# A hybrid decoder step on one core: residual rows turned by VectorE with short store runs, scores and splits in another order

## What is computed

```
h = rmsnorm(x); proj = h @ w_in                 # q,k,v,z_A,alpha,beta,u,z_B
o_a = gated delta rule (8 heads of 128)         # half of the mixing width
o_b = causal pooling over 2/4/8/16 positions    # the other half
x  = x + concat(o_a, o_b) @ w_out               # x2, the residual rows
h2 = rmsnorm(x); qx = h2 @ w_cq                 # 4 heads of 512
scores = qx @ mem_k; probs = softmax(scores)    # 256 memory tokens
x  = x + (probs @ mem_v) @ w_co
y  = rmsnorm(x)
```

## Time and profile before

| | |
|---|---|
| three runs, us | 1635.26, 1636.34, 1639.36 (median 1636.34) |
| profiled execution, us | 1636.29 |
| its span, first to last instruction, us | 1634.5 |
| busy in the span | PE 98%, PEld 88%, DVE 60%, ACT 40%, POOL 10% |
| granted TensorE clock, mean | 0.995 |
| DMA | 274.65 MB, mean 168 GB/s |

### The profile page before, as it was taken

One profiled execution on the slowest core, in us unless ns is written; L12 is line 12 of the kernel. 1 busy time (PEld: TensorE's weight loads), 2 busy tenths in 40 slices (PEclk: granted clock), 3 DMA queues, 4 the chain that ended last, 5 costly groups with the idle time before them and its releaser, 6 DMA issues.

```text
span 1634.5 us, 29970 instructions
## 1 busy us (share of the span) xinstructions
PE 1597.5 (98%) x12034; PEld 1441.9 (88%) x12034; DVE 978.8 (60%) x1669; ACT 647.0 (40%) x1110; POOL 155.7 (10%) x170
## 2 busy tenths in 40 slices
PE   7999999999999999999999999999999999999997
PEld 5887899999999999999999999999999996667655
DVE  5676447776857767667344563434688765532445
ACT  5666444343543434425322233323434325332422
POOL 0121000211121121211100011111000000000000
PEclk9999999999999999999999999999999999999999
DMA  7798744332342332424289946777613359977664
GB/s 270 247 293 260 238 132 119 79 94 75 97 111 60 99 98 70 115 52 131 77 194 232 248 134 169 221 217 217 166 57 99 104 175 335 333 246 250 222 222 161
DMA packets 318832, 274.65 MB, mean 168 GB/s; under 512 B 17402, under 2 KB 266115, under 8 KB 317715
## 3 DMA queue, kind: packets, MB, share of 16 engines
q1 hardware_dynamic: 296304, 256.48, 52.8%
q10 hardware_dynamic: 22434, 16.87, 3.8%
HBM read 229.49 MB, written 44.17 MB: 167 GB/s over the span
## 4 chain that ended last, share of the span: by engine, by line
PE 96%; DVE 2%; ACT 1%; DMA 0%; issue 0%; SPq 0%; ACTq 0%; DVEq 0%
PE pj L283 51%; PE pj L504 11%; PE dk L2998 6%; PE pj L2338 4%; PE dk L2338 3%; PE pj L2957 3%; PE pj L2965 2%; PE dk L2623 1%; DVE w_low_co L2557 1%; PE pj L2645 1%; PE pj L2662 1%; PE dk L1926 1%; PE dk L1303 1%; PE dk L366 1%; PE dk L1319 1%; PE dk L1419 1%
## 5 line engine op out<-in xcount | busy, mean ns | idle before, releaser
L283 PE MATMUL pj<-a_hi,w_high 128*128 128x272 f32 x1664 | 364.7, 300 | 0.0
L283 PE MATMUL pj<-a_hi,w_low 128*128 128x272 f32 x1664 | 343.6, 288 | 0.0
L283 PE MATMUL pj<-a_lo,w_high 128*128 128x272 f32 x1664 | 343.1, 288 | 0.0
L283 PEld LDWEIGHTS pj<-a_hi,w_high 128*128 128x128 f32 x1664 | 259.4, 189 | 12.3 <-issue 7.8
L283 PEld LDWEIGHTS pj<-a_lo,w_high 128*128 128x128 f32 x1664 | 261.5, 188 | 0.0
L283 PEld LDWEIGHTS pj<-a_hi,w_low 128*128 128x128 f32 x1664 | 260.0, 189 | 0.0
L267 DVE TENSOR_TENSOR w_low<-w_raw,w_high 128x2048 fp32r<-128x2048 f32 x68 | 155.3, 2284 | 85.4 <-ACT w_high L257 85.4
L257 ACT ACTIVATE w_high<-w_raw 128x2048 fp32r<-128x2048 f32 x68 | 130.4, 1917 | 75.1 <-PE pj L283 42.4
L283 PE MATMUL pj<-mix_hi,w_high 128*128 128x272 f32 x512 | 107.1, 290 | 0.0
L283 PE MATMUL pj<-mix_lo,w_high 128*128 128x272 f32 x512 | 105.7, 288 | 0.0
L283 PE MATMUL pj<-mix_hi,w_low 128*128 128x272 f32 x512 | 105.3, 287 | 0.0
(11 more groups left out here) (464 smaller groups left out, 2913.8 us busy)
## 6 DMA issues: line engine op xcount, KB each, us to landing
w_raw<-in_w_in_dram SPq DMA_DIRECT2D x48, 1024.0 KB, 6.0
w_raw_co<-in_w_co_dram SPq DMA_DIRECT2D x28, 1024.0 KB, 6.9
w_raw_wide<-in_w_ck_dram SPq DMA_DIRECT2D x16, 1024.0 KB, 9.6
w_raw_wide<-in_w_cv_dram SPq DMA_DIRECT2D x16, 1024.0 KB, 7.8
w_raw<-in_w_out_dram SPq DMA_DIRECT2D x16, 1024.0 KB, 7.9
keys_s<-keysT_scratch SPq DMA_DIRECT2D x7, 2048.0 KB, 10.7
values_s<-in_cache_mem_v_dram SPq DMA_DIRECT2D x28, 512.0 KB, 7.0
q_part<-in_w_cq_dram SPq DMA_DIRECT2D x48, 256.0 KB, 3.6
```

The costliest lines, as they stand in the source:

```text
L283: mm = pe.matmul(pj[:, 2 * (q % 2) + b, 0:n], wt[:, k, :], x(k, o, n), start=(k == 0 and m == 0), stop=(k == KT - 1 and m == 2))
```

## The change

1. *Residual rows.* PE's transposes (turn_x2), ACT's copies (act_x2) and the semaphore x2_taken are gone. DVE turns x2's 512 prompt columns in 32x32 blocks into xr, behind the requests' transpose. sp_x2 stores xr with four DMAs a tile, one for each 32 partitions, in runs of 32 floats. The residual load of tile i + 2 waits until tile i's store from the same buffer has landed (64 a tile on x2_stored), not for the sum's read. All later waits on x2_stored go from 128 to 512.
2. *Banks.* The scores of head 3 lie in dk banks 0 and 1, and wait for pt_low of head 0 only.
3. *Order of attention.* PE: scores 3 and the turn of head 2 go ahead of the requests' values of head 0, and the turn of these goes into unit 0. ACT and DVE: turned values of head 0 and 1 and weight tiles 0 and 1 are prepared earlier.
4. *Order of the products.* DVE splits tile w + 1 ahead of both products of w, and makes a request head's sums and the next head's queries ahead of products or rows. ACT takes the requests' context of head 0 between the products of tile 0.

```diff
@@ -1995,7 +1995,7 @@
             if 4 * j + q >= 2:
-                sp.wait_ge(pj_read, 80 + 4 * j + q - 1)
+                sp.wait_ge(x2_stored[q % 2], 64 * (2 * j + q // 2))
             sp.dma_start(xr[q % 2][:], xT_d[bass.ds(4 * j + q, 1), :, :].rearrange("k p n -> p (k n)")).then_inc(xr_loaded[q % 2], 16)
@@ -2017,30 +2017,15 @@
-            sp.wait_ge(x2_taken, i + 1)
-            sp.dma_start(x2_d[:, :, i * P:(i + 1) * P].rearrange("b p c -> p b c"),
-                         x2[i % 2][:, 0:SEQ].rearrange("p (b c) -> p b c", b=CH)).then_inc(x2_stored[i % 2], 16)
+            sp.wait_ge(x2_turned, i + 1)
+            rows = x2_d[:, :, i * P:(i + 1) * P].rearrange("n (q t) (a f) -> a t (n q) f", t=T32, f=T32)
+            for a in range(4):
+                sp.dma_start(rows[a], xr[i % 2][a * T32:(a + 1) * T32, 0:SEQ].rearrange("t (b f) -> t b f", f=T32)).then_inc(
+                    x2_stored[i % 2], 16)
             if i % 4 == 3:
...
                     sp.dma_start(x2s_d[:, i - 3:i + 1, a, :], xs_t[i // 4 % 2][a * NS:(a + 1) * NS]).then_inc(x2s_stored, 16)
-
-        def turn_x2(i, bank):
-
-            def step(pe):
-                pe.wait_ge(pj_read, 80 + i + 1)
-                at_least(pe, x2_taken, i - 3)
-                for b in range(CH):
-                    mm = pe.transpose(dk[:, bank, b * P:(b + 1) * P], x2[bank % 2][:, b * P:(b + 1) * P], ident)
-                mm.then_inc(x2_turned, 1)
-            return step
-
-        def act_x2(act, i):
-
-            act.wait_ge(x2_turned, i + 1)
-            act.wait_ge(h_low, i + 1)
-            act.wait_ge(sqx_ready, i + 1)
-            act.activation(x2[i % 2][:, 0:SEQ], dk[:, i % 4, :], ACT.Copy).then_inc(x2_taken, 1)
@@ -2050,8 +2035,6 @@
                     i = 4 * j + q
-                    if i > 0:
-                        act_x2(act, i - 1)
                     act.wait_ge(pj_read, 80 + i + 1)
@@ -2074,7 +2057,7 @@
                     dve.wait_ge(xr_loaded[q % 2], 32 * j + 16 * (q // 2) + 16)
-                    at_least(dve, x2_stored[q % 2], 32 * j + 16 * (q // 2))
+                    at_least(dve, x2_turned, i - 1)
                     at_least(dve, sqx_ready, i - 1)
@@ -2086,6 +2069,8 @@
                     dve.transpose(xs_t[j % 2][:, q, :], x2[q % 2][:, SEQ:TOK]).then_inc(xs_turned, 1)
+                    dve.wait_ge(pj_read, 80 + i + 1)
+                    dve.transpose(xr[q % 2][:, 0:SEQ], x2[q % 2][:, 0:SEQ]).then_inc(x2_turned, 1)
             for j in range(4):
@@ -2114,12 +2099,10 @@
                     pe.wait_ge(ust_ready, 8)
-                if q > 0:
-                    steps = {7: [turn_x2(q - 1, q - 1)]}
                 multiply(pe, "out", 0, q, tokens(mix_hi), tokens(mix_lo), TOK, steps)
...
                 for q in range(4):
-                    multiply(pe, "out", j, q, tokens(mix_hi), tokens(mix_lo), TOK, {7: [turn_x2(4 * j + q - 1, (q - 1) % 4)]})
+                    multiply(pe, "out", j, q, tokens(mix_hi), tokens(mix_lo))
@@ -2233,7 +2216,7 @@
                 for k in range(2):
-                    dve.wait_ge(x2_stored[k], 128)
+                    dve.wait_ge(x2_stored[k], 512)
                 dve.wait_ge(x2s_stored, 256)
@@ -2317,7 +2300,6 @@
                     pe.wait_ge(col2_root, 1)
-                    pe.wait_ge(x2_taken, 16)
             elif kh == 0 and o == 0:
@@ -2364,8 +2346,6 @@
                     cast_high(act, "cq", 0, q + 1)
-                if q == 0:
-                    act_x2(act, 15)
                 if q == 1:
@@ -2427,7 +2407,6 @@
             pe.wait_ge(acc_done, 16)
-            pe.wait_ge(x2_taken, 14)
             for i in range(4):
@@ -2435,7 +2414,7 @@
             multiply(pe, "cq", 0, 0, tokens(a_hi), tokens(a_lo), TOK,
-                     {7: [turn_x2(15, 3)], 14: [lambda pe: pe.wait_ge(h_low, 16)], 15: [lambda pe: token_sums(pe)]})
+                     {14: [lambda pe: pe.wait_ge(h_low, 16)], 15: [lambda pe: token_sums(pe)]})
             for q in range(1, 4):
@@ -2609,15 +2588,15 @@
-            return (dk[:, 0:2, :], dk[:, 2:4, :], pj[:, 0:2, :], dk[:, 2:4, :])[h]
+            return (dk[:, 0:2, :], dk[:, 2:4, :], pj[:, 0:2, :], dk[:, 0:2, :])[h]
...
             if h == 3:
-                pe.wait_ge(pt_high.sem, pt_high.at(2))
-                pe.wait_ge(pt_low.sem, pt_low.at(2))
+                pe.wait_ge(pt_high.sem, pt_high.at(1))
+                pe.wait_ge(pt_low.sem, pt_low.at(1))
             for i in range(4):
@@ -2680,11 +2659,10 @@
             pe_turn(pe, 1)
+            pe_prompt_scores(pe, 3)
+            pe_turn(pe, 2)
             pe_values(pe, 0, 0)
             pe_values(pe, 0, 1)
-            pe_prompt_scores(pe, 3)
-            pe_turn_values(pe, 0)
-            pe_turn(pe, 2)
@@ -2748,12 +2726,13 @@
             act_exps(act, 2)
-            act_values(act, 0)
             act_turned_values(act, 0)
             cast_product(act, 0)
-            act_context(act, 0)
             act_turned(act, 2)
             act_exps(act, 3)
+            act_values(act, 0)
+            act_turned_values(act, 1)
+            cast_product(act, 1)
@@ -2803,9 +2782,10 @@
             maxima(3)
+            split_product(dve, 0)
             dve_turned(dve, 2)
             over_sums(3)
-            split_product(dve, 0)
+            dve_turned_values(dve, 1)
@@ -2874,9 +2854,9 @@
                 w = TILE_UNITS.get(u)
-                if w is not None and w + 1 < TILES:
+                if w is not None and 1 < w + 1 < TILES:
                     cast_product(act, w + 1)
-                if u < XH - 1:
+                if 0 < u < XH - 1:
                     act_turned_values(act, u + 1)
@@ -2887,9 +2867,11 @@
                 if w is not None:
+                    if w == 0:
+                        act_turned(act, 3)
                     act_product(act, w, 0)
                     if w == 0:
-                        act_turned(act, 3)
+                        act_context(act, 0)
                     act_product(act, w, 1)
@@ -2920,21 +2902,21 @@
                 if step == 2:
                     probabilities(dve, h)
-                if u < XH - 1:
+                if 0 < u < XH - 1:
                     dve_turned_values(dve, u + 1)
-                if w is not None:
-                    dve_product(dve, w, 0)
-                    if w == 0:
-                        dve_turned(dve, 3)
-                    if w + 1 < TILES:
-                        split_product(dve, w + 1)
-                    dve_product(dve, w, 1)
-                else:
-                    dve_rows_unit(dve, u)
+                if w is not None and w + 1 < TILES:
+                    split_product(dve, w + 1)
                 if step == 1:
                     request_sums(dve, h)
                     if h + 1 < XH:
                         queries(dve, h + 1)
+                if w is not None:
+                    if w == 0:
+                        dve_turned(dve, 3)
+                    dve_product(dve, w, 0)
+                    dve_product(dve, w, 1)
+                else:
+                    dve_rows_unit(dve, u)
         def pe_products(pe):
@@ -3005,10 +2987,10 @@
                     if w == 0:
+                        pe_turn_values(pe, 0)
                         high_half(w, 1)
+                        pe_turn(pe, 3)
                     low_half(w, 0)
-                    if w == 0:
-                        pe_turn(pe, 3)
                     if AGAIN <= w + 1 < TILES:
```

More of the change, by code:

```diff
@@ L1964, in build @@
             "h_high", "h_low", "sqx_ready", "acc_zero", "acc_done"))
-        x2_turned, x2_taken, xs_turned, x2s_stored = (sem(n) for n in ("x2_turned", "x2_taken", "xs_turned", "x2s_stored"))
+        x2_turned, xs_turned, x2s_stored = (sem(n) for n in ("x2_turned", "xs_turned", "x2s_stored"))
         xs_t = [put(f"xs_t{i}", [4, NS], F32, M_W - 272 + i * 4 * NS) for i in range(2)]
@@ L2350, in sp_cq @@
             for i in range(2):
-                sp.wait_ge(x2_stored[i], 128)
+                sp.wait_ge(x2_stored[i], 512)
             sp.wait_ge(sums_done, 1)
@@ L2815, in build @@
         gain_loaded, xs_loaded = Reused(old_rows, 16), Reused(mst_stored, 128)
-        x_half_loaded = [Reused(x2_stored[i], 128) for i in range(2)]
+        x_half_loaded = [Reused(x2_stored[i], 512) for i in range(2)]
         (out_done, row_added, row_squared, row_summed, row_root, row_over, row_gained, row_scaled_a, row_scaled_v, s_added) = (
@@ L3161, in sp_rows_out @@
             for s, v in ((mst_stored, 128), (kts_stored, 128), (xts_stored, 80), (st_stored, 768), (s_stored, 128),
-                         (s0_stored, 128), (ust_stored, 16 * 72), (old_rows, 16), (x2_stored[0], 128), (x2_stored[1], 128),
+                         (s0_stored, 128), (ust_stored, 16 * 72), (old_rows, 16), (x2_stored[0], 512), (x2_stored[1], 512),
                          (x2s_stored, 256)):
```

## The result

The changed kernel takes **1621.73 us** (median of 4 runs, 1620.14 to 1623.8), the kernel before beside it 1635.8 (4 runs, 1635.1 to 1639.36): a ratio of 0.9911, interval 0.9899 to 0.9923. The forecast was 1618 in a range of 1608 to 1630. The profiled execution took 1621.54 us, 1.7 more than its span.

The account below looks back on a forecast made before the run. PE was taken to bound the kernel, busy 1597.5 of 1634.5 us. Terms -7.0 - 5.4 - 3.4 - 3.2 + 0.6 = -18.4 took 1636.3 to 1618 us, range 1608 to 1630.

Parts of the forecast that it names:

- Part 1, PE's work: Output and query stages: PE loses 64 transposes, sixteen groups of 0.44 us, for -7.0 us.
- Part 1, the added wait: Output stage: residual load waits for the store's landing, about one us late, unseen by PE; price 0, bounds 0 and +15.
- the slack of 3.7 us: Output stage: time free between the end of DVE's low-part split and PE's need for it, 3.7 us.
- second rival: Output stage: loads landing 26.5 us behind the add delay each tile pair 2.5 us; 15 us, 1633 us; chance 0.22.
- Its milder reckoning: Output stage, second rival: one us lost per pair of tiles instead of 2.5, for 1622 us.
- Part 2: Output tiles 12 to 15: split first closes three 1.80 us waits, -5.4 us; half-clock stretches disappear, -3.4 us.
- Part 3: Later attention units: requests' sums first closes two of three waits for probabilities, -3.2 us.
- Part 4: Turn from attention to products: waits close, but late weights 3 cost PE 5 to 7 us; +0.6 instead of -9.1.
- first rival: Turn to products: the queue makes up its delay, loads aren't late, part 4 brings -9.1; 1608 us; chance 0.18.
- third rival: Output stage: 128-byte writes cost 54 ns beside weight loads, DMA sets the stage, +43 us; 1668 us; chance 0.06.
- the turning point: Output stage, third rival: the change turns slower at 39 ns a packet, where a tile needs over 13.15 us.
- fourth rival: DVE's new order exposes another equal wait and the clock falls; only part 1 left, 1629 to 1634; chance 0.06.

Follow-up runs that it names:

- Split first alone: Kernel before with only DVE's split of tile w + 1 ahead of both products of w, for w from 1 on: 1628.1 us, ratio 0.9943.
- the sums alone: Kernel before with only DVE's requests' sums and next head's queries ahead of products or rows: 1630.96 us, ratio 0.9956.
- (store): Changed kernel with SP storing a tile's turned residual rows before it waits for the turned keys: 1619.32 us, ratio 0.9899.
- (residual load): Changed kernel with the residual load issued ahead of the weight load, from the second tile on: 1618.59 us, ratio 0.9883.
- (weights 2): Changed kernel with weights 2 and turned values 3 loaded ahead of head 1's first keys: 1619.75 us, ratio 0.9905.
- (rows): Changed kernel with the 2 MB load of residual rows behind weights 3 instead of ahead: 1616.58 us, ratio 0.9878.
- all together: Changed kernel with residual load before weights, store before keys, weights 2 and values 3 before head 1's keys, 2 MB rows behind weights 4: 1608.07 us, ratio 0.982.
- part 1 alone: Kernel before with only the block transposes in the out stage, old attention order: 1632.1 us, ratio 0.997.

## Why the prediction was right, and where it was off

**The sum.** -3.3 + 1.7 - 3.6 - 9.6 = -14.8 against -18.4: right in sign and in the range, 3.7 us too good. One term of part 1 has all of it. The other misses, +1.1 in part 4, -0.4 in part 3 and -0.8 in part 2, cancel each other, and that is luck.

**Part 1, PE's work: right.** Sixteen groups at 0.44 us were to bring 7.0; with the loads in time the run gave 7.1.

**Part 1, the added wait: the step that failed** is "one us late. PE doesn't see it ... Price 0". It measured 3.85 us. In the round shown the way to the load was right within 0.2 us (store 14.5 us behind the sum for 14.65, load at 20.1 for 20.1). Two things were not. The load took 6.1 us beside the weights, so it landed at 26.2 and not at 25. And the slack of 3.7 us was charged once, though the lateness of one round is handed to the next: against a grid of 12.0 us from the first sum (979.90), the sums of tiles 5, 7 and 9 came 1.3, 2.3 and 4.6 us late (1041.20, 1066.18, 1092.47), and with the third the slack was used up. A loop whose rounds are longer than their period on average has no slack; it only takes a number of turns to show.

That is the second rival's mechanism, with 3.85 us in place of its 15. Its round of 26.5 us was nearly right for a long round (26.3 and 26.8), but it took every round to be one, and the others took 23.8 to 25.0: over the five rounds from tile 5 on the mean is 25.2. Only two tiles made PE stand. Its milder reckoning, one us a pair, gave 7.5 - 3.7 = 3.8 us and 1622, and 3.85 and 1621.7 came, closer than the 2 us to which this term is known, so in part luck. So the outcome is the forecast's for parts 2 to 4 and for PE's work in part 1, and the second rival's for the added wait.

**Part 2: right, by both of its terms.** Split first alone gave 9.4 us from tile 12 on, waits and clock together; forecast 5.4 + 3.4.

**Part 3: right.** Forecast 3.2, measured 3.6; the sums alone remove the three waits.

**Part 4: the mechanism right, one size off.** The keys load left 3.3 us later than before, at 1377.64; in the time of the kernel before (3.3 us are part 1's) that is 1380.9, forecast 1381.1. Weights 3 landed at 1405.2 + 3.3 = 1408.5, forecast 1407.5, and PE started tile 3 at 1412.8, forecast 1411.6. The mis-sized term is the share of the delay that the queue would make up: 1.3 of 6.8 us were allowed for, 0.3 came. From the issue of the keys load to the landing of weights 3 it was 27.5 us, as before (27.7: 1374.32 to 1402.0), with the same 7.5 MB of loads between them; with the 2 MB of rows moved behind weights 3 it was 22.4.

The clock fell twice, where one stretch was forecast, but the first (from 1396.1) lay ahead of the long wait and only made that wait shorter: it cost nothing. The second, from 1406.3 to 1413.2, overlapped 3.7 us of work behind the wait and cost half of it, 1.8 us, for 1.7. The first rival (loads not late) fell with the 5.56 us wait; orders that land weights 3 earlier against the first scores, after 65.6, 62.9, 60.4 and 56.5 us, bring the request turn after 77.1, 74.3, 73.0 and 67.3 us, so the landing sets it, except that at 60.4 another wait had taken over. By that row most of that rival's -9.1 was there to be had: 67.3 is 8.1 less than the 75.4 of before.

**The third rival fell.** DMA queues from 1000 to 1100 us, to be read against the earlier trace rows:

```profile
q1 hardware_dynamic: 42528, 16.87, 68.0%
q10 hardware_dynamic: 6730, 4.11, 15.0%
```

The share grew by 7.3 and 0.7 points, not to near 1. The first queue's 7.3 points are 7.3% x 16 x 100 / 8.33 = 14.0 us of engine time a tile; with the removed 512 packets at the mix's 33 ns (an estimate) the 2048 new ones took (14.0 + 16.9) / 2048 = 15 ns each beside weight loads, where 39 (38 by its own terms) would have been the turning point. The rule that was weighed there, from the Trainium skill, "DMA: Bandwidth & Descriptors", Specifications (under 512 bytes not at line rate), gives no size; here the rows show such packets at 13 ns almost alone and, by that estimate, 15 beside weight loads. The mix before moved 16.71 MB in 29689 packets, 563 bytes each, in 33 ns, so a byte in a 128-byte packet took 1.7 to 2 times as long (an estimate): the direction of the rule is borne out, and the output stage didn't feel it: with the residual load ahead of the weights its tiles last 12.00 us.

**The fourth rival fell** with the last window of the result: no PE wait and the full clock from 1413.2 to 1614.

## What to carry to other kernels

When a change makes a buffer serve twice (load, store, load again), write down the whole round, from use to use, and compare it with the period; if it is longer by one microsecond on average, slack of four is spent in four rounds, so never charge it once. Count what comes only every few turns too. Of loads on one queue, put those that are wanted soonest and are smallest first: 272 KB behind 1 MB took twice as long to land, and 2 MB that nobody needed yet held up 1 MB that PE was waiting for. And before an instruction is moved on a compute engine, look which load waits for it and how full the queue is behind that load.

## What the runs showed beyond what was expected

- **The order of issues was worth as much as the change.** The same work with the DMA issues in another order went from 1621.7 to 1608.1 us. By the ratios to the kernel before, the single edits gave 2.0 (store), 4.6 (residual load), 1.0 (weights 2) and 5.4 us (rows) over the changed kernel; each ratio is known to some 2 us, so the first and the third are not clear of noise as times. The sum of the two of the attention stage and the larger of the other two is 11.0, less than the 14.9 of all together (where the rows go one load further back, and no stretch at 1.2 GHz is left).
- **A full queue.** Weights 3, 1 MB, landed 18.0 us after their issue in the changed kernel and 9.1 in the kernel before, though the DMA share was 1.04 between issue and landing in both; they were issued 2.4 us earlier than there (1387.17 + 3.3 against 1392.8) and landed 6.5 us later. The other orders gave 19.7, 16.7 and 13.3 us at shares of 1.02 to 1.04. So the share doesn't tell when a load lands; what is still ahead of it does. The same 7.5 MB stood ahead of weights 3 in both kernels, from the keys load on, issued within 9.5 us in the changed one and 18.5 before.
- **The same wait, another clock.** A wait of 2.4 us in tile 0 was followed by a stretch at 1.2 GHz in the kernel before and by none with part 1 alone, and the three waits of 1.80 us by two such stretches in the kernel before, with the sums first and with part 1 alone. The wait of 1.83 us in tile 1, with the splits first, and those of 1.96 us for the probabilities were followed by none. So the clock's share of a gain is not to be had from the length of one wait.
- **Executions differ in the output stage.** The same out stage lost 3.1 us in PE's waits in the changed kernel's execution, 1.7 in that with weights 2 first and 4.3, the first query tiles included, in that with the rows later, so a term of this kind is known to some 2 us only. DVE's sums can stand still in the old output stage too: with the splits or the sums first they did so for 18.3 and 15.6 us between 1000 and 1200 (no releaser shown), though never in the trace of the kernel before; PE had no wait in the 16 output tiles there.
